# Causal term of the decay arguments on VectorE from head 2 on, and the sample tile's final scaling behind two bank reads

## The chip, the cores and the metric

The kernel runs on one core of a Trainium2 chip. The metric is the device time of one execution in microseconds (us). Of the engines, TensorE (PE in the profile) does matmuls and transposes into eight PSUM banks, VectorE (DVE) and ScalarE (ACT) read those banks, GpSimd (POOL) works on SBUF and issues DMAs, and SyncE (SP) issues most other DMAs. Each engine runs its instructions in program order, and semaphores order the engines among each other.

## The reference, cut to what matters

One step of a hybrid decoder layer: a short gated convolution and an mLSTM matrix memory read the same normalised input and write through one output projection. 2048 prompt tokens (with 16 meta tokens in front) and 64 sample tokens (8 sequences of 8) go through it. The change touches the decay weights of the mLSTM:

```python
log_d = jnp.where(causal, b[..., :, None] - b[..., None, :] + ig[..., None, :], -jnp.inf)
m_t = jnp.maximum(m_inter, jnp.max(log_d, axis=-1))
d = jnp.exp(log_d - m_t[..., None])
inter = jnp.exp(m_inter - m_t)
s = jnp.einsum('bhjd,bhsd->bhjs', q, k) * d
num = jnp.einsum('bhjs,bhsv->bhjv', s, v) + inter[..., None] * jnp.einsum('bhjd,bhdv->bhjv', q, c_prev)
```

and the last normalisation of the sample output:

```python
out = jnp.einsum('btw,wd->btd', jnp.concatenate([y_conv, y_m], axis=-1), w_out)
y_sample = rmsnorm(x + out, final_norm_gain)
```

## The kernel before, in words

**Stages.** A prologue transposes and splits the input. The main part goes over 4 heads (`g` = 0 to 3), each with 4 blocks (`b` = 0 to 3) of 512 tokens (4 chunks of 128); `n = 4 g + b` counts the blocks. "Head 2" is `g` = 1. In a block, nine tiles of projection columns follow each other in the order K, V, Q, GC, HC, GB, ZC, O, ZM. A tile is 24 matmuls of 512 columns, since both operands are split into two f16 parts and three products are taken for each of 8 slices (lines 732 to 734). V is built from 96 matmuls of 128 columns (lines 741 to 743). With `b` = 0 a small mixed piece (meta and sample tokens, 80 columns) comes ahead of each tile.

**Decay factors.** At the end of tile Q, TensorE writes into bank `A` the product of a row selector `selneg` and `mparts` (the running maximum in three bf16 parts, line 849), adds the causal mask on top by a second matmul (`identb` times the mask `maskb`, line 850), and writes the first product once more, without the mask, into bank `N[0]` (line 853). ScalarE makes `dp` = exp(A + column 3 of `sel`) and `eh` = exp(N[0] + column 4), four instructions each, one for a chunk. VectorE then multiplies `eh` by `qf`. At the end of the next tile, GC, TensorE writes the scores into bank `S` (line 860) and VectorE multiplies `dp` by them. From the middle of tile ZC on, TensorE takes the chunks (lines 809, 810 and 815) that need both. `dp` has held the block before's head output until then: it may be overwritten once GpSimd has made its four sums of it (semaphore `y_sums`, line 603).

**The end of the program.** After the last block, TensorE multiplies the sample rows by the output weights (lines 965, 966) into banks `T1` and `PB[0]`, and then does the prompt's output projection: 8 units of 256 rows, each with seven products of 12 matmuls (lines 978 to 980; a Strassen form with the operand sums S1 to S4). In unit 0 the order is A11 of unit 0, S2, S1, A12, S3, A11 of unit 1, A22, S4. A product goes into one of three banks of a chain, `one`, `two`, `three`. S3 adds to bank `two` what S2 left there, after VectorE has read it (`add_bank(..., s6_out, ...)`, which also waits for the first of three additions that GpSimd makes in `residuals`). A22 waits for `u7_out` in the same way, S4 for `c22_out`.

VectorE adds the sample banks to `zsmp` (four instructions), then takes the mean of squares of the sample tile (`b_mean(0, ...)`, after ScalarE's `b_square`), waits for GpSimd's power of -0.5 (`b_power(0, ...)`) and scales (`b_final(0, ...)`), and only then turns to unit 0. GpSimd's own order there is: the four sums of the last block, `residuals(0)`, `store_sums`, two small stores, `b_power(0, ...)`, a wait for `b_out`, the store of `y_sample`, and then `residuals(1)`.

VectorE and ScalarE issue through a helper, so all their instructions show as line 160; they are told apart by their tiles.

Of the kernel before, what the change touches and what calls it, by code (L numbers as in the profile page):

```python
# [33 lines left out]
ALU = mybir.AluOpType  # L34
ACT = mybir.ActivationFunctionType

P = 128
# [4 lines left out]
DB, DS = 8, 8  # L42
# [121 lines left out]
def build(nc, x_prompt, x_sample, state_conv, state_c, state_n, state_m, meta, norm_gain, w_in, conv_w,  # L164
# [3 lines left out]
    with ctx:  # L168
# [5 lines left out]
        def sem(name):  # L174
            return ctx.enter_context(nc.semaphore(name))
# [88 lines left out]
        def w_pair(w, t):  # L264
# [25 lines left out]
        t0_full, t0_free, t1_full, t1_free = sem("t0_full"), sem("t0_free"), sem("t1_full"), sem("t1_free")  # L290
        a_full, a_free, s_full, s_free = sem("a_full"), sem("a_free"), sem("s_full"), sem("s_free")
        e_full, e_ready, n_full, n_free = sem("e_full"), sem("e_ready"), sem("n_full"), sem("n_free")
        g_logits, g_abs, g_exp, g_ln, rows_ready = (
            sem(n) for n in ("g_logits", "g_abs", "g_exp", "g_ln", "rows_ready"))
        sel_ready, q_scaled, gc_used = sem("sel_ready"), sem("q_scaled"), sem("gc_used")
# [429 lines left out]
        def _(pe):  # L725
# [113 lines left out]
            def at_end(g, b, t, first):  # L839
                n = nth(g, b)  # L840
                if first:
                    for r in X_END.get(t, ()):
                        x_round(1 + CH * (b + 1) + r // 2, r % 2, t0(g, b, ("x", r), first))
                if t == Q:

                    pe.wait_ge(sel_ready, n + 1)
                    pe.wait_ge(a_free, n * 3)
                    m = mparts[:, tok0(b):tok0(b) + BT]
                    mm(A[:, :], selneg[:, :], m, start=True, stop=False)
                    mm(A[:, :], identb[:, :], maskb[:, :].unsqueeze(1).broadcast_to([P, CH, P]), start=False, stop=True)\  # L850
                        .then_inc(a_full, 1)
                    pe.wait_ge(n_free, n)
                    mm(N[0][:, :], selneg[:, :], m, start=True, stop=True).then_inc(e_full, 1)
                if t == GC:
                    bank_, left = evacuations(g, b, Q)
                    pe.wait_ge(p_free[bank_], left + 1)
                    pe.wait_ge(s_free, n * 3)
                    for c in range(CH):
                        cc = slice(c * P, (c + 1) * P)
                        last = mm(S[:, cc], kf[:, cc], qf[:, cc], start=True, stop=True)  # L860
                    last.then_inc(s_full, 1)
                if t == ZC:
                    chunk(g, b, 1, first)
                if t == O:
                    chunk(g, b, 3, first)
                if b == 0:
                    mixed_end(g, b, t, first)
                if b == 1 and t in (V, Q, GC):
                    i0, i1 = SAMPLE_ROUNDS[t - V]
                    pe.wait_ge(mx_v_wide, g + 1)  # L870
                    use_t1(t1(g, b, ("state", t - V), first))
                    mm(T1[:, 0:(i1 - i0) * DV1], kwm[:, :], v1x[:, i0:i1, :].rearrange("p b v -> p (b v)"),
                       start=True, stop=True).then_inc(t1_full, 1)
                if first and t == ZC:
                    gates(2 + 2 * CH * (b + 2), tok0(b + 1), BT, t1(g, b, "gates", first))
                if first and b == NB - 2 and t == ZM:
                    columns(b + 3, BT, t1(g, b, "next cols", first))
# [149 lines left out]
        def _(act):  # L1027
# [149 lines left out]
            def at_end(g, b, t, first):  # L1177
                n = nth(g, b)
                if t == Q:
                    act.wait_ge(ym_low, n)  # L1180
                    act.wait_ge(y_sums, 4 * n)
                    act.wait_ge(sel_ready, n + 1)

                    for out, src, kind, full, free, value in ((dp, A, 3, a_full, a_free, n * 3 + 1),
                                                              (eh, N[0], 4, e_full, e_ready, n + 1)):
                        act.wait_ge(full, value)
                        for c in range(CH):
                            cc = slice(c * P, (c + 1) * P)
                            last = fn(out[:, cc], src[:, cc], ACT.Exp, bias=sel[:, c, kind:kind + 1])
                            if c < CH - 1:  # L1190
                                did(last)
                        mark(last.then_inc(free, 1), free, value)
# [147 lines left out]
        def _(dve):  # L1340
# [242 lines left out]
            def select(g, b, first):  # L1583

                n = nth(g, b)
                if first and b == 0:
                    dve.wait_ge(const2, 1)
                if first or b == NB - 1:
                    dve.wait_ge(t1_free, COLS_COUNTS[b + 1] + 1)
                dve.wait_ge(tile_done, n * NT + 1)  # L1590
                dve.wait_ge(e_ready, n)
                if b == 0:
                    factors(g)
                mark(pick(sel[:, :, :], cols[:, 1 + CH * b:1 + CH * (b + 1), :, bass.ds(g, 1)].rearrange("p c k o -> p c (k o)"))
                     .then_inc(sel_ready, 1), sel_ready, n + 1)
# [11 lines left out]
            def at_end(g, b, t, first):  # L1607
# [1 line left out]
                if t == K and not first:  # L1609
                    select(g, b, first)  # L1610
                if t == Q:
                    dve.wait_ge(e_ready, n + 1)
                    mark(tt(eh[:, :], eh[:, :], qf[:, :], ALU.mult).then_inc(q_scaled, 1), q_scaled, n + 1)
                if t == GC:
                    dve.wait_ge(s_full, n * 3 + 1)
                    dve.wait_ge(a_free, n * 3 + 1)
                    mark(tt(dp[:, :], dp[:, :], S[:, :], ALU.mult).then_inc(s_free, 1), s_free, n * 3 + 1)
                if t == ZC:
                    dve.wait_ge(a_free, n * 3 + 2)
# [181 lines left out]
            def b_mean(tile, n):  # L1801

                dve.wait_ge(b_sq, tile + 1)
                mark(ts(msx[0:n, tile:tile + 1], ssx[0:n, tile:tile + 1], 1.0 / D, EPS, ALU.mult, ALU.add).then_inc(b_ms, 1), b_ms, tile + 1)

            def b_final(tile, z, n):

                dve.wait_ge(b_rs, tile + 1)
                mark(stt(z, z, rsx[0:n, tile:tile + 1], fgain[0:n, :], ALU.mult, ALU.mult).then_inc(b_out, 1), b_out, tile + 1)
# [6 lines left out]
            for h in range(2):  # L1816
# [2 lines left out]
                add_bank(z, SMP[h][0:n, :], smp_added, 2 * h + 1)  # L1819
                dve.wait_ge(smp_added, 2 * h + 1)  # L1820
                add_bank(z, SMP[h][n:2 * n, :], smp_added, 2 * h + 2)
            b_mean(0, n)
            dve.wait_ge(fg_in, 16)
            b_final(0, zsmp[0:n, :], n)
            for n in range(UNITS):
                z1, z2 = Z[n % 2]
                one, two, three = CHAINS[n % 2]
# [3 lines left out]
                if n:  # L1831
                    b_mean(2 * n, P)
                    b_final(2 * n - 1, Z[1 - n % 2][1], P)
                if n < UNITS - 1:
                    dve.wait_ge(prod_done, p2_done(n))
                    add_bank(z1[:, 0:BT], one[:, :], c11_out, n + 1)
# [7 lines left out]
                if n == UNITS - 1:  # L1844
                    dve.wait_ge(prod_done, p2_done(n))
                    add_bank(z1[:, 0:BT], one[:, :], c11_out, n + 1)
                dve.wait_ge(prod_done, p4_done(n))
                add_bank(z2[:, 0:BT], two[:, :], c21_out, n + 1)
                b_mean(1 + 2 * n, P)
# [42 lines left out]
```

## Time and profile before

| | |
|---|---|
| median of 3 runs | 1156.07 us (1153.03 to 1157.19) |
| the profiled execution's own time | 1155.46 us |
| its span | 1153.7 us |
| TensorE busy | 1095.1 us, 95% |
| VectorE busy | 519.4 us, 45% |
| ScalarE busy | 354.1 us, 31% |
| GpSimd busy | 249.9 us, 22% |

Engine times are from one profiled execution. The span runs from its first to its last recorded work, and the execution's own time is 1.76 us longer. A matmul's duration holds the fill and drain of the array, which overlap the next matmul: the distance from one start to the next is what it takes of the engine. The clock that TensorE was granted is given as a share of full speed.

### The profile page before, as it was taken

To read this page: it belongs to the slowest core of one execution; us is meant where nothing else is said; L and a number is where in the kernel's file an instruction comes from. 1 tells how busy PE (TensorE), PEld (TensorE's weight loads), DVE (VectorE), ACT (ScalarE), POOL (GpSimd) and SP (SyncE) were. 2 spreads that over 40 slices of the span, in tenths; PEclk is the share of its full clock that TensorE was granted. 3 is DMA by queue.
4 is the path that set the end of the run, shared out by engine and by line. 5 is a ranking of instruction groups with operands and counts; after the bars stand their busy time and mean duration, and the time that the engine had idled before them with its cause. 6 is when DMAs were issued, how large, how long until landed. Compare 5 with 4: busy or idle time off the path is not lost. (4 is left out here: it accounts for less than half of the span.)

```text
span 1153.7 us, 18272 instructions
## 1 busy us (share of the span) xinstructions
PE 1095.1 (95%) x7274; PEld 622.3 (54%) x7274; DVE 519.4 (45%) x1045; ACT 354.1 (31%) x701; POOL 249.9 (22%) x332
## 2 busy tenths in 40 slices
PE   3888999989999999999999999999999999799996
PEld 3555645545566555556565655566656555344442
DVE  5756665575533443454343424544432223334333
ACT  5563354625321323243222223422222131121211
POOL 5000220202020223120213131211211121433322
PEclk9989999999999999999999999999999999899998
DMA  5231020005220021173101314410212062246652
GB/s 179 76 109 43 12 92 23 29 23 136 82 83 7 16 87 61 47 198 87 38 7 48 87 43 125 139 35 20 91 37 88 23 210 88 103 146 229 220 209 90
DMA packets 89048, 100.02 MB, mean 87 GB/s; under 512 B 7248, under 2 KB 73956, under 8 KB 88964
## 3 DMA queue, kind: packets, MB, share of 16 engines
q1 hardware_dynamic: 49024, 58.06, 15.7%
q0 software_dynamic: 7600, 25.03, 6.0%
q10 hardware_dynamic: 32340, 15.78, 5.1%
q8 instruction: 57, 0.93, 0.3%
q14 instruction: 27, 0.22, 0.1%
HBM read 65.43 MB, written 33.41 MB: 86 GB/s over the span
## 5 line engine op out<-in xcount | busy, mean ns | idle before, releaser
L733 PE MATMUL bank<-xTl,Wh 128*128 128x512 f16 (+1 forms) x1280 | 420.9, 345 | 0.0
L732 PE MATMUL bank<-xTh,Wh 128*128 128x512 f16 (+1 forms) x1280 | 418.2, 345 | 2.4 <-DVE xtmp L160 2.4
L734 PE MATMUL bank<-xTh,Wl 128*128 128x512 f16 (+1 forms) x1280 | 420.2, 345 | 0.0
L734 PEld LDWEIGHTS bank<-xTh,Wl 128*128 128x128 f16 x1280 | 126.5, 99 | 121.9 <-issue 1.9
L732 PEld LDWEIGHTS bank<-xTh,Wh 128*128 128x128 f16 x1280 | 126.4, 99 | 110.7 <-issue 4.5
L733 PEld LDWEIGHTS bank<-xTl,Wh 128*128 128x128 f16 x1280 | 126.5, 99 | 108.9 <-issue 3.1
L741 PE MATMUL bank<-Wh,xTh 128*128 128x128 f16 x544 | 94.1, 221 | 4.2 <-DVE ysum L160 3.9
L743 PE MATMUL bank<-Wh,xTl 128*128 128x128 f16 x544 | 94.1, 221 | 0.0
L742 PE MATMUL bank<-Wl,xTh 128*128 128x128 f16 x544 | 94.1, 221 | 0.0
L160 ACT ACTIVATE tz<-bank 128x512 f32<-128x512 f32 x32 | 19.1, 598 | 134.7 <-PE bank L734 133.9
L160 DVE SCALAR_TENSOR_TENSOR Wl<-wst,Wh 128x1024 f16<-128x1024 f32 x36 | 46.1, 1282 | 29.1 <-ACT Wh L160 26.9
L741 PEld LDWEIGHTS bank<-Wh,xTh 128*128 128x128 f16 x544 | 53.7, 99 | 7.6 <-DVE ysum L160 5.4
L610 POOL TENSOR_TENSOR ysumst<-ysum,ysumst 128x1024 f16<-128x1024 f32 x16 | 34.1, 2132 | 95.2 <-ACT ysumst L160 95.2
L742 PEld LDWEIGHTS bank<-Wl,xTh 128*128 128x128 f16 x544 | 53.7, 99 | 1.6
L743 PEld LDWEIGHTS bank<-Wh,xTl 128*128 128x128 f16 x544 | 53.7, 99 | 0.0
L594 POOL DMA_DIRECT2D y_ops<-yst x16 | 11.8, 738 | 187.4 <-DVE yst L160 187.4
L160 DVE SCALAR_TENSOR_TENSOR cn<-cn,sel,bank 128x129 f32<-128x129 f32 x64 | 22.4, 350 | 62.9 <-PE bank L815 59.0
L160 DVE SCALAR_TENSOR_TENSOR xs<-bank,xs 128x512 f32<-128x512 f32 x36 | 24.9, 692 | 52.8 <-PE bank L980 52.1
L160 DVE TENSOR_TENSOR eh<-eh,qf 128x512 f32<-128x512 f32 x16 | 11.1, 692 | 80.9 <-ACT eh L160 80.9
L592 POOL DMA_DIRECT2D y_ops<-yst x16 | 11.9, 743 | 161.3 <-DVE yst L160 161.3
L160 ACT ACTIVATE Wh<-wst 128x1024 f16<-128x1024 f32 x36 | 38.0, 1057 | 26.4 <-PE bank L734 18.4
L763 PE MATMUL bank<-ident,xs 128*128 128x128 f32 (+1 forms) x136 | 24.7, 323 | 20.1 <-DVE xs L160 10.0
(313 smaller groups left out, 1602.1 us busy)
## 6 DMA issues: line engine op xcount, KB each, us to landing
xs<-in_x_prompt SPq DMA_DIRECT2D x28, 512.0 KB, 3.9
wst<-in_w_in ACTq DMA_DIRECT2D x27, 512.0 KB, 4.6
y_ops<-ysumst POOLq DMA_DIRECT2D x16, 512.0 KB, 3.2
w_ops<-xs SPq DMA_DIRECT2D x16, 448.0 KB, 3.8
out<-xs POOLq DMA_DIRECT2D x11, 512.0 KB, 2.9
Wh<-y_ops SPq DMA_DIRECT2D x12, 448.0 KB, 3.5
Wl<-y_ops SPq DMA_DIRECT2D x12, 448.0 KB, 4.3
wst<-in_w_in SPq DMA_DIRECT2D x9, 512.0 KB, 4.2
```

Source lines behind the costliest of these rows:

```text
L160: return op(*operands, **named)
L592: pool.dma_start(ops[:, :, A12 * 2 * P:(A22 + 1) * 2 * P], src).then_inc(out, 16)
L594: pool.dma_start(ops[:, :, 0:2 * P], src[:, :, 0:2 * P]).then_inc(out, 16)
L610: pool.tensor_tensor(parts[:, :, 1, :], ysum[:, :, :, :].rearrange("p r o t -> p (r o) t"), parts[:, :, 0, :], ALU.subtract).then_inc(y_su ...
L732: mm(out, wh[:, k, :], xh, start=(k == 0), stop=False)
L733: mm(out, wh[:, k, :], xl, start=False, stop=False)
L734: last = mm(out, wl[:, k, :], xh, start=False, stop=(k == KT - 1))
L741: mm(out, xh, Wh[:, V, k, :], start=(k == 0), stop=False)
L742: mm(out, xh, Wl[:, V, k, :], start=False, stop=False)
L743: last = mm(out, xl, Wh[:, V, k, :], start=False, stop=(k == KT - 1))
L763: last = nc.tensor.transpose(bank_[:, k * n:k * n + n], xs[unit % XBUF][0:n, (4 * r + k) * P:(4 * r + k + 1) * P], ident[0:n, 0:n])
```

## The change

Three things change. For `g` >= 1 the mask matmul and the second matmul of `selneg` go: TensorE writes only the plain product into bank `A`. VectorE adds the mask to it and writes the sum to `dp` in SBUF (a new semaphore, `arg_ready`). ScalarE then makes `eh` first, from bank `A`, and `dp` second, in place from SBUF (a new semaphore, `dp_ready`). Head 1 (`g` = 0) keeps the old form. VectorE rather than ScalarE now waits for `y_sums` there. At the end of the program, `b_mean(0, ...)` moves behind the read of bank `two` of unit 0, and `b_final(0, ...)` behind that unit's three other reads `c11_out`, `u7_out` and `c22_out`.

```diff
--- before.py
+++ after.py
@@ -290,6 +290,7 @@
         t0_full, t0_free, t1_full, t1_free = sem("t0_full"), sem("t0_free"), sem("t1_full"), sem("t1_free")
         a_full, a_free, s_full, s_free = sem("a_full"), sem("a_free"), sem("s_full"), sem("s_free")
         e_full, e_ready, n_full, n_free = sem("e_full"), sem("e_ready"), sem("n_full"), sem("n_free")
+        arg_ready, dp_ready = sem("arg_ready"), sem("dp_ready")
         g_logits, g_abs, g_exp, g_ln, rows_ready = (
             sem(n) for n in ("g_logits", "g_abs", "g_exp", "g_ln", "rows_ready"))
         sel_ready, q_scaled, gc_used = sem("sel_ready"), sem("q_scaled"), sem("gc_used")
@@ -846,11 +847,14 @@
                     pe.wait_ge(sel_ready, n + 1)
                     pe.wait_ge(a_free, n * 3)
                     m = mparts[:, tok0(b):tok0(b) + BT]
-                    mm(A[:, :], selneg[:, :], m, start=True, stop=False)
-                    mm(A[:, :], identb[:, :], maskb[:, :].unsqueeze(1).broadcast_to([P, CH, P]), start=False, stop=True)\
-                        .then_inc(a_full, 1)
-                    pe.wait_ge(n_free, n)
-                    mm(N[0][:, :], selneg[:, :], m, start=True, stop=True).then_inc(e_full, 1)
+                    if g:
+                        mm(A[:, :], selneg[:, :], m, start=True, stop=True).then_inc(a_full, 1)
+                    else:
+                        mm(A[:, :], selneg[:, :], m, start=True, stop=False)
+                        mm(A[:, :], identb[:, :], maskb[:, :].unsqueeze(1).broadcast_to([P, CH, P]), start=False, stop=True)\
+                            .then_inc(a_full, 1)
+                        pe.wait_ge(n_free, n)
+                        mm(N[0][:, :], selneg[:, :], m, start=True, stop=True).then_inc(e_full, 1)
                 if t == GC:
                     bank_, left = evacuations(g, b, Q)
                     pe.wait_ge(p_free[bank_], left + 1)
@@ -1177,13 +1181,18 @@
             def at_end(g, b, t, first):
                 n = nth(g, b)
                 if t == Q:
-                    act.wait_ge(ym_low, n)
-                    act.wait_ge(y_sums, 4 * n)
                     act.wait_ge(sel_ready, n + 1)
-
-                    for out, src, kind, full, free, value in ((dp, A, 3, a_full, a_free, n * 3 + 1),
-                                                              (eh, N[0], 4, e_full, e_ready, n + 1)):
-                        act.wait_ge(full, value)
+                    if g:
+                        act.wait_ge(arg_ready, n + 1 - NB)
+                    else:
+                        act.wait_ge(ym_low, n)
+                        act.wait_ge(y_sums, 4 * n)
+                        act.wait_ge(a_full, n * 3 + 1)
+
+                    for out, src, kind, free, value in ((eh, A, 4, a_free, n * 3 + 1), (dp, dp, 3, dp_ready, n + 1 - NB)) if g else (
+                            (dp, A, 3, a_free, n * 3 + 1), (eh, N[0], 4, e_ready, n + 1)):
+                        if src is N[0]:
+                            act.wait_ge(e_full, n + 1)
                         for c in range(CH):
                             cc = slice(c * P, (c + 1) * P)
                             last = fn(out[:, cc], src[:, cc], ACT.Exp, bias=sel[:, c, kind:kind + 1])
@@ -1588,7 +1597,10 @@
                 if first or b == NB - 1:
                     dve.wait_ge(t1_free, COLS_COUNTS[b + 1] + 1)
                 dve.wait_ge(tile_done, n * NT + 1)
-                dve.wait_ge(e_ready, n)
+                if n <= NB:
+                    dve.wait_ge(e_ready, n)
+                else:
+                    dve.wait_ge(dp_ready, n - NB)
                 if b == 0:
                     factors(g)
                 mark(pick(sel[:, :, :], cols[:, 1 + CH * b:1 + CH * (b + 1), :, bass.ds(g, 1)].rearrange("p c k o -> p c (k o)"))
@@ -1609,11 +1621,21 @@
                 if t == K and not first:
                     select(g, b, first)
                 if t == Q:
-                    dve.wait_ge(e_ready, n + 1)
+                    if g:
+                        dve.wait_ge(a_full, n * 3 + 1)
+                        dve.wait_ge(y_sums, 4 * n)
+                        mark(tt(chunks(dp[:, :]), chunks(A[:, :]), maskb[:, :].unsqueeze(1).broadcast_to([P, CH, P]), ALU.add)
+                             .then_inc(arg_ready, 1), arg_ready, n + 1 - NB)
+                        dve.wait_ge(a_free, n * 3 + 1)
+                    else:
+                        dve.wait_ge(e_ready, n + 1)
                     mark(tt(eh[:, :], eh[:, :], qf[:, :], ALU.mult).then_inc(q_scaled, 1), q_scaled, n + 1)
                 if t == GC:
                     dve.wait_ge(s_full, n * 3 + 1)
-                    dve.wait_ge(a_free, n * 3 + 1)
+                    if g:
+                        dve.wait_ge(dp_ready, n + 1 - NB)
+                    else:
+                        dve.wait_ge(a_free, n * 3 + 1)
                     mark(tt(dp[:, :], dp[:, :], S[:, :], ALU.mult).then_inc(s_free, 1), s_free, n * 3 + 1)
                 if t == ZC:
                     dve.wait_ge(a_free, n * 3 + 2)
@@ -1819,9 +1841,7 @@
                 add_bank(z, SMP[h][0:n, :], smp_added, 2 * h + 1)
                 dve.wait_ge(smp_added, 2 * h + 1)
                 add_bank(z, SMP[h][n:2 * n, :], smp_added, 2 * h + 2)
-            b_mean(0, n)
             dve.wait_ge(fg_in, 16)
-            b_final(0, zsmp[0:n, :], n)
             for n in range(UNITS):
                 z1, z2 = Z[n % 2]
                 one, two, three = CHAINS[n % 2]
@@ -1831,6 +1851,8 @@
                 if n:
                     b_mean(2 * n, P)
                     b_final(2 * n - 1, Z[1 - n % 2][1], P)
+                else:
+                    b_mean(0, DB * DS)
                 if n < UNITS - 1:
                     dve.wait_ge(prod_done, p2_done(n))
                     add_bank(z1[:, 0:BT], one[:, :], c11_out, n + 1)
@@ -1844,6 +1866,8 @@
                 if n == UNITS - 1:
                     dve.wait_ge(prod_done, p2_done(n))
                     add_bank(z1[:, 0:BT], one[:, :], c11_out, n + 1)
+                if n == 0:
+                    b_final(0, zsmp[0:DB * DS, :], DB * DS)
                 dve.wait_ge(prod_done, p4_done(n))
                 add_bank(z2[:, 0:BT], two[:, :], c21_out, n + 1)
                 b_mean(1 + 2 * n, P)
```

TensorE, end of tile Q in the last block of the last head. Before:

```order
L734 MATMUL bank<-xTh,Wl 128x512
L849 MATMUL bank<-mparts,selneg 128x512
L850 MATMUL bank<-maskb,identb 128x512
L853 MATMUL bank<-mparts,selneg 128x512
L732 MATMUL bank<-xTh,Wh 128x512
L733 MATMUL bank<-xTl,Wh 128x512
```

And now, where every line number of TensorE is one or two higher:

```order
L735 MATMUL bank<-xTh,Wl 128x512
L851 MATMUL bank<-mparts,selneg 128x512
L733 MATMUL bank<-xTh,Wh 128x512
L734 MATMUL bank<-xTl,Wh 128x512
L735 MATMUL bank<-xTh,Wl 128x512
```

Two of the three matmuls between tile Q and tile GC are gone; nothing else moved on TensorE.

VectorE, tiles V to GC of the last block, as a piece of the difference (`maskb` is the mask):

```order
 L160 TENSOR_TENSOR yst<-dp,yst 128x4x128
 L160 TENSOR_TENSOR kw<-bank,sel 128x512
+L160 TENSOR_TENSOR dp<-bank,maskb 128x512
 L160 TENSOR_TENSOR eh<-eh,qf 128x512
 L160 TENSOR_TENSOR dp<-dp,bank 128x512
```

One instruction was added, between the scaling of K and the product with Q.

VectorE, from the last head output on (`wst` 64x... is the sample tile, `xs` the output rows of unit 0, `prow` the small outputs). Before:

```order
L160 MEMSET den 128x1
L160 SCALAR_TENSOR_TENSOR wst<-bank,wst 64x512 x4
L160 TENSOR_SCALAR msx<-ssx 64x1
L160 SCALAR_TENSOR_TENSOR wst<-wst,rsx,fgain 64x1024
L160 SCALAR_TENSOR_TENSOR xs<-bank,xs 128x512 x5
L160 TENSOR_SCALAR msx<-ssx 128x1
L160 SCALAR_TENSOR_TENSOR xs<-bank,xs 128x512
```

And now:

```order
L160 MEMSET den 128x1
L160 SCALAR_TENSOR_TENSOR wst<-bank,wst 64x512 x4
L160 SCALAR_TENSOR_TENSOR xs<-bank,xs 128x512
L160 TENSOR_SCALAR msx<-ssx 64x1
L160 SCALAR_TENSOR_TENSOR xs<-bank,xs 128x512 x3
L160 SCALAR_TENSOR_TENSOR wst<-wst,rsx,fgain 64x1024
L160 SCALAR_TENSOR_TENSOR xs<-bank,xs 128x512
L160 TENSOR_SCALAR msx<-ssx 128x1
```

The mean of the sample tile now stands behind the first bank read of unit 0, and its scaling behind the fourth.

## Rows read from the trace of the kernel before

**Rows 1.** The page, part 1: busy us, share of the span, instructions.

```profile
PE 1095.1 (95%) x7274; PEld 622.3 (54%) x7274; DVE 519.4 (45%) x1045; ACT 354.1 (31%) x701; POOL 249.9 (22%) x332
```

**Rows 2.** Busy us (instructions) in a stretch: PE, PEld, DVE, ACT, POOL, clock, DMA.

```profile
520.00:740.00 220.00, 218.84 (x1563) 128.07 (x1562) 91.04 (x192) 65.14 (x137) 49.05 (x57) 1.00 0.24 72
```

**Rows 3.** Waits of TensorE: us in total, times, longest.

```profile
PE bank L978 <- DVE xs L160: 7.0, 1, 7.0
...
PE bank L790 <- DVE dp L160: 1.7, 2, 1.2
```

**Rows 4.** Timeline of TensorE, a Q end: start, us, engine, line.

```profile
944.12 0.38 PE L849 MATMUL bank<-mparts,selneg 68*128 68x512 bf16 x1
...
944.56 0.38 PE L853 MATMUL bank<-mparts,selneg 68*128 68x512 bf16 x1
944.78 0.38 PE L732 MATMUL bank<-xTh,Wh 128*128 128x512 f16 x1
```

**Rows 5.** Line 850 from 300 to 960 us: ns min/median/max, first and last.

```profile
L850 PE MATMUL bank<-maskb,identb x12: 379/379/380, 333.0 to 944.3; 128*128 128x512 bf16 x12
```

**Rows 6.** Timeline of an ordinary block (head 2, third block), by engine.

```profile
448.24 1.57 ACT L160 ACTIVATE dp<-bank,sel 128x128 f32<-128x128 f32 x4
...
451.50 0.69 DVE L160 TENSOR_TENSOR eh<-eh,qf 128x512 f32<-128x512 f32 x1 [5.87 <-ACT eh L160]
454.26 0.69 DVE L160 TENSOR_TENSOR dp<-dp,bank 128x512 f32<-128x512 f32 x1 [2.06 <-PE bank L860]
...
467.01 0.39 PE L809 MATMUL bank<-v,dp 128*128 128x129 f32 x2
```

**Rows 7.** Timeline of head 2's fourth block, by engine.

```profile
503.41 1.57 ACT L160 ACTIVATE dp<-bank,sel 128x128 f32<-128x128 f32 x4 [2.63 <-POOL ysum L603]
...
509.09 0.60 ACT L160 ACTIVATE gcs<-bank 128x512 f32<-128x512 f32 x1
...
509.20 0.69 DVE L160 TENSOR_TENSOR dp<-dp,bank 128x512 f32<-128x512 f32 x1
...
511.89 0.38 PE L732 MATMUL bank<-xTh,Wh 128*128 128x512 f16 x1
...
519.66 0.39 PE L809 MATMUL bank<-v,dp 128*128 128x129 f32 x2
```

**Rows 8.** Timeline of TensorE around the end's longest wait.

```profile
998.63 0.38 PE L980 MATMUL bank<-xTh,Wl 128*128 128x512 f16 x1
1005.98 0.61 PE L978 MATMUL bank<-xTh,Wh 128*128 128x512 f16 x1 [6.96 <-DVE xs L160]
...
1010.19 0.38 PE L978 MATMUL bank<-Wh 128*128 128x512 f16 x1
...
1012.78 0.38 PE L978 MATMUL bank<-xTh,Wh 128*128 128x512 f16 x1
```

**Rows 9.** Timeline of VectorE in the same stretch.

```profile
991.08 3.06 DVE L160 SCALAR_TENSOR_TENSOR wst<-bank,wst 64x512 f32<-64x512 f32 x4
997.37 0.15 DVE L160 TENSOR_SCALAR msx<-ssx 64x1 f32<-64x1 f32 x1 [3.23 <-ACT junk L160]
1003.82 1.27 DVE L160 SCALAR_TENSOR_TENSOR wst<-wst,rsx,fgain 64x1024 f32<-64x1024 f32 x1 [6.30 <-POOL rsx L685]
1005.23 1.49 DVE L160 SCALAR_TENSOR_TENSOR xs<-bank,xs 128x512 f32<-128x512 f32 x2
```

**Rows 10.** Timeline of GpSimd in the same stretch.

```profile
995.09 3.72 POOL L680 TENSOR_TENSOR xs<-xs,xtmp 128x512 f32<-128x512 f32 x3
998.76 2.13 POOL L610 TENSOR_TENSOR ysumst<-ysum,ysumst 128x1024 f16<-128x1024 f32 x1
...
1003.12 0.60 POOL L685 TENSOR_TENSOR rsx<-msx,halves 64x1 f32<-64x1 f32 x1
1005.40 0.60 POOL L702 DMA_DIRECT2D out<-wst  x1 [1.68 <-DVE wst L160]
```

**Rows 11.** As in rows 2, a stretch behind the long wait.

```profile
1005.00:1010.00 5.00, 4.02 (x12) 1.50 (x13) 1.48 (x3) 0.00 (x0) 0.60 (x1) 0.57 0.24 52
```

## The prediction

> **What bounds the kernel now.** I read the page's busy shares first. TensorE is busy for 1095.1 of 1153.7 us, VectorE for under half [rows 1]. An average can hide a stage with another limit, so I took the busy times by stage next: in 520 to 740 us TensorE is busy for 218.84 of 220 us at full granted clock, VectorE for 91.04 [rows 2]. In heads 2 to 4 the time is therefore what TensorE has to issue, and an instruction taken from it should come back whole. Then the list of TensorE's waits: apart from the first 300 us, which the change leaves as they are, it holds two short ones of together 1.7 us (line 790, for `dp`), and one of 7.0 us, the longest of all, in front of a product of line 978 [rows 3]. That one is the second place where time can be had. The timelines of three engines around it say what it waits for.
>
> **Part 1, two matmuls less in each block of heads 2 to 4.** Line 850 ran 12 times in those heads [rows 5], line 853 once beside it each time, so 24 matmuls go. What one takes of TensorE is the distance between starts: from 944.12 (line 849) two starts on to 944.56 (line 853) and one more to 944.78, so 0.22 us each, not the 0.38 us in the duration column [rows 4]. 24 x 0.22 = 5.3 us. Charging the duration would give 24 x 0.38 = 9.1 us; I leave that out of the range's centre because the next matmul started while the last was still draining.
>
> The Trainium skill ("TensorE: Matmul & The Clock Gate", "Wait — 56ns, not 53.3ns?") puts back-to-back matmuls of 512 columns at 215.7 ns from start to start. As an estimate by that page the 24 would be 5.2 us; the same page's duration of a matmul would not be the price.
>
> **What VectorE gets for it.** Twelve additions `dp<-bank,maskb` of 128x512. The trace has none with a mask operand in bf16; the nearest row is the product `dp<-dp,bank` of the same size, also with one PSUM operand, at 0.69 us [rows 6]. That is 12 x 0.69 = 8.3 us of VectorE in all. In an ordinary block it stood idle for 5.87 us ahead of `eh<-eh,qf` [rows 6], and the addition lies in exactly that idle time. Even at three times 0.69 us it would fit. Cost on the path: 0, bound above only by the cover below.
>
> **The new order of hands.** Before: ScalarE made `dp` (1.57 us) and `eh` (as long), and VectorE went on at 451.50, 3.26 us after ScalarE's start at 448.24 [rows 6]. Now: addition 0.69, `eh` 1.57, and VectorE can go on, while ScalarE makes `dp` for another 1.57. With ScalarE's start at 448.24 as before (the addition runs while it still copies Q out), `eh` times `qf` comes at about 449.9 instead of 451.5, and `dp` is ready at about 451.6. The product with the scores stood at 454.26, released by TensorE [rows 6], so it does not move. Its first user, line 809, started at 467.01, that is 12.1 us after the product's end at 454.95 [rows 6].
>
> The tighter case is the fourth block of heads 2 and 3, where GpSimd is late with its sums and ScalarE waited 2.63 us for them before `dp` at 503.41 [rows 7]. There the addition can't start before 503.4, so ScalarE starts 0.7 to 0.8 us later than before, and so does all behind it in its queue: a weight split, a copy of sums, and `gcs<-bank` at 509.09 to 509.69. The last of them frees the bank that tile GB needs; GB started at 511.89 [rows 7]. The copy would end at 510.5, so 1.4 us are left, 1.0 us when TensorE is 0.44 us earlier. VectorE's product with the scores would slip from 509.20 to about 510, still 9 us ahead of line 809 at 519.66 [rows 7]. Cost: 0; if that cover were gone, two blocks x 0.8 us = 1.6 us at most. The two waits of line 790 hang on VectorE's work since the end of the block before, not on the Q end, and stay at 1.7 us [rows 3]. They could also hide one block's gain each, so I put part 1 between 5.3 - 1.6 = 3.7 us and 5.3 us and take 5.3.
>
> The Trainium skill ("PSUM — Partial Sum Buffer", "PSUM bank collisions raise a hardware error") says that two engines must not read one bank in the same partitions at once. Bank `A` now has two readers, so they must stand in a row, and `arg_ready` puts them so. By that rule the 0.7 us of the addition can't be overlapped with `eh`. That waiting is what rival B below lives on: without the rule it would have no chance at all, with it a small one. No run here shows such a collision.
>
> **Part 2, the sample tile's scaling.** TensorE's last matmul before the wait started at 998.63 and would have let the next one start at 998.85. It started at 1005.98 [rows 8]: 7.13 us lost. VectorE is the reason. Its four sample additions ended at 994.14. It waited 3.23 us for ScalarE's squares, took the mean at 997.37, waited 6.30 us for GpSimd's power, scaled from 1003.82 to 1005.09, and read the bank for S3 only at 1005.23 [rows 9]. GpSimd was late because its power stood behind `residuals(0)` (995.09 to 998.81), `store_sums` (998.76 to 1000.89) and stores, and ran at 1003.12 [rows 10].
>
> Now the bank read comes first. It needs S2, which ended two products of 2.59 us before 998.85, so at 993.7, and the first of GpSimd's three additions, 995.09 + 3.72/3 = 996.33 [rows 10]. A product at full speed takes 1012.78 - 1010.19 = 2.59 us [rows 8]. The read runs from about 996.4 to 997.2 (0.75 us, half of the pair at 1005.23 [rows 9]). TensorE wants it at 998.85, so 1.6 us are left over, and the wait goes.
>
> What is late next? After the gap the twelve matmuls of S3 took 1010.19 - 1005.98 = 4.21 us instead of 2.59 [rows 8], because a good part of them ran at the lower of the two granted clock levels, 1.2 instead of 2.4 GHz: the clock of 1005 to 1010 us is a mean of 0.57 of full speed, and the first matmul shows 0.61 us instead of 0.38 [rows 8, 11]. Without the gap nothing lets the clock fall: another 1.62 us. Part 2 is then 7.13 + 1.62 = 8.75 us. The next waits: S3 ends at 1001.44, VectorE reads for A22 until 1002.4 and for S4 until 1003.2, and TensorE wants them at 1004.03 and 1006.62 (A11 of unit 1 lies between), so no wait. The sample scaling then waits for the power at 1003.72 and runs to 1005.1, before A22 ends at 1006.6: hidden. GpSimd issues the store of the sample rows behind it (0.60 us [rows 10]) and is free for `residuals(1)` at 1005.9; the first of its additions ends at 1007.1, and the read that needs it can't come before S2 of unit 1 ends, five products of 2.59 us after 998.85, at 1011.8. About 4.7 us are left.
>
> The Trainium skill ("TensorE: Matmul & The Clock Gate", "Part 1: The HAM clock gate (the "warmup" mystery)") says that the length of the slow stretch after a pause varies from run to run with where the pause falls. By that rule the 1.62 us is one draw, and in the median run the gain of part 2 could be 7.1 us plus less or more than that; the profiled run alone can't tell.
>
> **The sum.** 5.3 + 8.75 = 14.0 us. Against the profiled execution's own 1155.46 us that is 1141.4; that execution is 0.61 us under the median of 1156.07, against which it is 1142.0. I forecast 1141.8 us.
>
> **Rivals.**
> A: the wait at the end only changes its name. For: S3 needs GpSimd too, and its margin is 1.6 us, on a queue where four sums stand ahead of `residuals(0)`. Against: GpSimd's rows there don't depend on anything that the change moves. If all of part 2 were lost, 5.3 us would be left: 1150.5 us.
> B: VectorE's longer chain eats part 1. For: the late blocks. Against: 12.1 and 9 us of cover. Then 8.75 us are left: 1147.0 us.
> C: slower. The point from which it decides is the cover ahead of line 809 in an ordinary block: 2.7 us from `dp` ready at 451.6 to the product with the scores, and 12.1 us behind that. If addition, `eh` and `dp` in a row were longer by more than 14.8 us, each microsecond beyond it would stop TensorE in 10 blocks. To reach 1162 us, 20 us would have to be lost, 2 us in each of them: the addition would take 14.8 + 2 + 0.7 = 17.5 us in place of 0.69. No row comes near it.
> D: the change does not do what it says, for example if the stop of line 978 was not VectorE's read but something else that came last. Then 1150 us or above, with A's price. The semaphore `s6_out` and the row at 1005.23 speak against it; I count it with A.
>
> **How the numbers follow.** Forecast 0.88, A with D 0.05, B 0.05, C 0.02. A measurement of this kernel can tell about 0.5%, 5.8 us, from no change. Forecast and B are faster by more than that; A, at 5.6 us under the median, is just within it. So faster 0.93, same 0.05, slower 0.02. The forecast's own range: from part 1 at 3.7 and part 2 at 7.13 (11 us, 1145) to the full 14.0, with the 2 us by which single runs of before lay around their median: 1139.5 to 1145.5 us. That leaves about 2 in 10 outside, most of it the other cases.
>
> **What would show it.** In the profile after: TensorE's wait list without the 7.0 us at line 978's successor; 24 matmuls less; S3's twelve matmuls at 2.59 us; the sample scaling behind four reads and ahead of TensorE's next need; VectorE's idle time ahead of `eh<-eh,qf` turned into a wait for bank `A`, the addition of 0.69 us and a shorter wait. Busy TensorE from 300 to 960 us should drop by 5.3 us in length and keep its share. Wrong would be: a new wait of TensorE for `gcs`, for `dp`, or for GpSimd's `xs`; an addition of over 1 us; or a clock under 1.00 between 990 and 1010 us.

## Result: 1140.8 us, ratio 0.987

| | before | after |
|---|---|---|
| median | 1155.92 us (4 runs) | 1140.84 us (4 runs, 1138.38 to 1141.35) |
| ratio | | 0.9869 (95% interval 0.9845 to 0.9892) |
| profiled execution, own time | 1155.46 us | 1141.35 us |
| span | 1153.7 us | 1139.6 us |

The kernel became 15.1 us faster by the medians and 14.1 us by the two profiled executions. The prediction had 1141.8 us, and 1141.4 us for an execution like the profiled one.

The page of the changed kernel, part 1, answers to [rows 1]:

```profile
PE 1088.8 (96%) x7250; PEld 620.0 (54%) x7250; DVE 529.7 (46%) x1057; ACT 355.7 (31%) x701; POOL 250.0 (22%) x332
```

24 matmuls are gone and 12 instructions of VectorE have come. The list of TensorE's waits from 300 us on, which answers to [rows 3], has lost the one of 7.0 us:

```profile
PE bank L791 <- DVE dp L160: 1.4, 2, 0.7
```

TensorE at the Q end, as in [rows 4] (columns: start, us, engine, line): one matmul in 0.22 us where three took 0.66.

```profile
939.21 0.38 PE L851 MATMUL bank<-mparts,selneg 68*128 68x512 bf16 x1
939.43 0.38 PE L733 MATMUL bank<-xTh,Wh 128*128 128x512 f16 x1
```

The ordinary block of [rows 6], VectorE and then ScalarE of the changed kernel:

```profile
447.14 0.69 DVE L160 TENSOR_TENSOR dp<-bank,maskb 128x512 f32<-128x512 f32 x1 [2.12 <-PE bank L851]
449.51 0.69 DVE L160 TENSOR_TENSOR eh<-eh,qf 128x512 f32<-128x512 f32 x1 [1.69 <-ACT eh L160]
453.21 0.69 DVE L160 TENSOR_TENSOR dp<-dp,bank 128x512 f32<-128x512 f32 x1 [3.00 <-PE bank L864]
```

```profile
447.91 1.57 ACT L160 ACTIVATE eh<-bank,sel 128x128 f32<-128x128 f32 x4 [0.40 <-DVE dp L160]
449.51 1.70 ACT L160 ACTIVATE dp<-dp,sel 128x128 f32<-128x128 f32 x4
```

The idle time of 5.87 us ahead of `eh<-eh,qf` has become a wait of 2.12 us for bank `A`, the addition, and a wait of 1.69 us. The product with the scores is still released by TensorE.

The end, as in [rows 8 to 10]; first VectorE, then TensorE, then GpSimd:

```profile
991.21 0.69 DVE L160 SCALAR_TENSOR_TENSOR xs<-bank,xs 128x512 f32<-128x512 f32 x1 [2.41 <-PE bank L984]
992.03 0.15 DVE L160 TENSOR_SCALAR msx<-ssx 64x1 f32<-64x1 f32 x1
...
996.29 1.49 DVE L160 SCALAR_TENSOR_TENSOR xs<-bank,xs 128x512 f32<-128x512 f32 x2 [1.90 <-PE bank L984]
998.42 1.28 DVE L160 SCALAR_TENSOR_TENSOR wst<-wst,rsx,fgain 64x1024 f32<-64x1024 f32 x1 [0.63 <-POOL rsx L686]
1001.47 0.69 DVE L160 SCALAR_TENSOR_TENSOR xs<-bank,xs 128x512 f32<-128x512 f32 x1 [1.78 <-PE bank L984]
```

```profile
993.29 0.38 PE L984 MATMUL bank<-xTh,Wl 128*128 128x512 f16 x1
993.50 0.38 PE L982 MATMUL bank<-xTh,Wh 128*128 128x512 f16 x1
```

```profile
1000.61 1.28 POOL L681 TENSOR_TENSOR xs<-xs,xtmp 128x512 f32<-128x512 f32 x1
```

The bank read ends at 991.90, and S3 starts at 993.50 right behind the product ahead of it, so 1.6 us were to spare. The sample scaling lies between the fourth read and the fifth, whose matmuls it doesn't hold up.

**Where the time came from.** I cut each trace at four marks: the first matmul of line 849 (851 after) in head 2, the last one in head 4, the start of unit 0's first product, and the last start of line 978 (982 after).

| us | first mark at | heads 2 to 4, to the second | to the third | products, to the fourth | rest |
|---|---|---|---|---|---|
| before | 332.8 | 611.3 | 44.4 | 153.2 | 12.0 |
| after | 333.1 | 606.1 | 43.9 | 144.5 | 12.0 |
| difference | +0.3 | -5.2 | -0.4 | -8.7 | 0 |

The differences are rounded after the subtraction. The third stretch holds the Q end of the last block, and so two of the 24 matmuls: together the matmul part gave 5.6 us.

### The profile page after: what moved, and what is told of

Same layout as the page of the kernel before. It is cut to its first block and busy times, and to the rows that moved or that the text cites. A ratio compares the mean times of both kernels' runs of the same rounds, so it can differ in the third digit from the quotient of the medians.

```text
span 1139.6 us, 18225 instructions
## 1 busy us (share of the span) xinstructions
PE 1088.8 (96%) x7250; PEld 620.0 (54%) x7250; DVE 529.7 (46%) x1057; ACT 355.7 (31%) x701; POOL 250.0 (22%) x332
## 5 line engine op out<-in xcount | busy, mean ns | idle before, releaser
L658 POOL TENSOR_TENSOR hrs<-hms,halves 128x4 f32<-128x4 f32 x16 | 16.5, 1032 | 112.6 <-DVE hms L160 112.6
```

Of the source, the lines that this page charges most:

```text
L658: pool.tensor_tensor(hrs[:, :], hms[:, :], halves[:, :], ALU.pow).then_inc(h_rs, 1)
```

## Experiments

Every kernel ran beside the kernel before on the same chip, on three chips in all. Each ratio is to that kernel's runs there (medians 1153.0, 1154.7 and 1154.4 us), and the differences in us below go by the ratios; "heads" and "products" are the stretches of the table above.

### The two parts alone

`tail_only` is the kernel before with part 2 alone:

```diff
-            b_mean(0, n)
             dve.wait_ge(fg_in, 16)
-            b_final(0, zsmp[0:n, :], n)
@@ behind the read of unit 0 for S3
+                else:
+                    b_mean(0, DB * DS)
@@ behind the reads for A22 and S4
+                if n == 0:
+                    b_final(0, zsmp[0:DB * DS, :], DB * DS)
```

> The kernel before with part 2 alone: the sample tile's mean and scaling behind the bank reads, all matmuls kept. Theory (the two parts add up, 7.13 us of wait and 1.62 us of low clock): 8.75 us less, 1147.2 us against 1155.9 of the kernel before. Rival A (GpSimd or another wait takes its place): above 1152 us. If the clock's 1.6 us does not come back: 1148.8 us. In the profile TensorE has no wait in front of S3 and its twelve matmuls take 2.6 us.

Measured: 1144.18 us, ratio 0.9927 (0.9910 to 0.9944), 8.4 us less. Heads 611.5, products 144.5, the same as after. Nothing took the place of the wait.

`mask_only` is the changed kernel with those lines put back as they were:

```diff
+            b_mean(0, n)
             dve.wait_ge(fg_in, 16)
+            b_final(0, zsmp[0:n, :], n)
@@
-                else:
-                    b_mean(0, DB * DS)
@@
-                if n == 0:
-                    b_final(0, zsmp[0:DB * DS, :], DB * DS)
```

> The changed kernel without part 2: two matmuls less in each of twelve blocks, VectorE adds the mask; the sample tile is scaled ahead of the bank reads as before. Theory (TensorE's issue is the bound, 0.216 us a matmul): 5.2 to 5.7 us less than the kernel before, 1150.4 us. Rival B (VectorE's longer chain eats it): 1154 to 1156 us. If a matmul cost its duration of 0.38 us: 9.1 us less, 1146.8 us.

Measured: 1149.11 us, ratio 0.9964 (0.9950 to 0.9978), 4.2 us less. Heads 606.3 and the third stretch 0.4 us less, so 5.4 us came from the matmuls. The products took 154.35 us, 1.1 more than the 153.25 before. The pause ahead of S3 is the same, 7.1 us, but the granted clock of 0.50 lasted until 5.5 us into the work behind it, and until 3.3 us into it in the profile before. TensorE, S3's first matmul and the first of the next product:

```profile
998.01 0.61 PE L982 MATMUL bank<-xTh,Wh 128*128 128x512 f16 x1 [6.95 <-DVE xs L160]
...
1003.11 0.60 PE L982 MATMUL bank<-Wh 128*128 128x512 f16 x1
```

S3 took 5.10 us here and 4.21 in [rows 8], 2.59 at full clock. The two parts add up to 12.6 us by the ratios; their intervals reach to the 14 to 15 us of the whole. In the traces, where the clock's draw can be set apart, they are 5.4 and 8.7 us.

### What the price of a matmul is

`more_matmuls`: the changed kernel with eight more of the same matmul at each Q end of heads 2 to 4.

```diff
                     if g:
+                        for _ in range(8):
+                            mm(A[:, :], selneg[:, :], m, start=True, stop=True)
                         mm(A[:, :], selneg[:, :], m, start=True, stop=True).then_inc(a_full, 1)
```

> The changed kernel with eight more matmuls of the same 512 columns into bank A at the end of tile Q in heads 2 to 4 (96 in all; each overwrites the last, so the output stays). If a matmul costs the distance between starts, 0.216 us: 20.7 us more than the changed kernel, 1161.5 us. If it costs its duration of 0.38 us: 36.5 us more, 1177.3 us. If other engines set part of the time: clearly under 20 us more.

Measured: 1162.23 us, ratio 1.006 (1.0041 to 1.0079), 22 us above the changed kernel. Heads 628.7, that is 22.6 us more, of which 2.0 are the longer waits below (1.4 us in the changed kernel); 20.6 are left for the matmuls. 20.7 us were expected from the distance between starts, 36.5 from the duration.

```profile
PE bank L791 <- DVE dp L160: 3.4, 2, 2.5
```

### What stopped TensorE at the end

`mean_ahead`: the changed kernel with `b_mean(0, ...)` ahead of the reads again, only `b_final(0, ...)` behind them.

```diff
+            b_mean(0, n)
             dve.wait_ge(fg_in, 16)
@@
-                else:
-                    b_mean(0, DB * DS)
```

> The changed kernel with only the scaling of the sample tile behind the bank reads; its mean of squares (which waits for ScalarE) stands ahead of them as before. Before, VectorE waited 3.2 us for ScalarE's squares and 6.3 us for GpSimd's power. If the wait for the power alone is what stopped TensorE: the same time as the changed kernel, 1140.8 us, since the mean would end at about 0.7 us before the time at which the read must start. If the squares' wait counts too: a wait of TensorE of up to 1 us and 1141 to 1142 us, more if the clock falls as well.

Measured: 1139.09 us, ratio 0.9882 (0.9868 to 0.9896); products 144.5. VectorE:

```profile
989.50 0.14 DVE L160 TENSOR_SCALAR msx<-ssx 64x1 f32<-64x1 f32 x1 [3.22 <-ACT junk L160]
989.78 0.69 DVE L160 SCALAR_TENSOR_TENSOR xs<-bank,xs 128x512 f32<-128x512 f32 x1
```

The read runs from 989.78 to 990.47, and S3 starts at 990.98 without a wait. Only the wait for GpSimd's power stopped TensorE; moving the mean was not needed.

`fill_wait`: the kernel before with 30 matmuls, whose result nobody uses, in the wait.

```diff
+                if n == 0:
+                    pe.wait_ge(t0_free, t0(H, 0, "hT", False) - t0_uses(0, False).index("hT") + 1)
+                    for i in range(30):
+                        mm(T0[:, :], yops[0][i % H][:, 0:P], w_operand(xTh, i % H, B_11), start=True, stop=True)
                 pe.wait_ge(s6_out, n + 1)
```

> The kernel before with 30 idle matmuls into the free bank T0 ahead of S3 of unit 0 (30 x 0.216 = 6.5 us in a wait of 7.13 us); their result is used by nobody. The wait itself stays. Theory (1.62 us of the 8.75 us are the low clock behind the pause): S3's twelve matmuls take 2.6 us and the time falls by 1.6 us to 1154.3 us. Rival (the low clock has another cause, or costs nothing on the path): 1155.9 us, no change.

Measured: 1153.53 us, ratio 0.9986 (0.9975 to 0.9998); products 151.6 instead of 153.2. TensorE, the last filler, S3's first and the next product's first:

```profile
1002.72 0.38 PE L1012 MATMUL bank<-Wh,Wl 128*128 128x512 f16 x1
1003.58 0.39 PE L978 MATMUL bank<-xTh,Wh 128*128 128x512 f16 x1 [0.49 <-DVE xs L160]
...
1006.18 0.38 PE L978 MATMUL bank<-Wh 128*128 128x512 f16 x1
```

S3 takes 2.60 us, so 1.6 us of part 2 were the clock and 7.1 the wait itself.

`power_first`: the kernel before, GpSimd's power moved up.

```diff
             residuals(0)
+            b_power(0, DB * DS)
             store_sums(H - 1, NB - 1)
@@
-            b_power(0, DB * DS)
             pool.wait_ge(b_out, 1)
```

> The kernel before with GpSimd's power of the sample tile moved ahead of its sums' store and two small stores (it runs at about 998.8 instead of 1003.1 us). VectorE's order is as before. Theory (the wait is VectorE's queue behind GpSimd's queue): the scaling runs from 999.5 to 1000.8, the read until 1001.6, so TensorE waits some 2.8 us instead of 7.1: 4.3 us less. If the clock stays up over the shorter pause, 1.6 us more of gain: 1150.0 us; if it still falls: 1151.6 us. Rival (something else releases S3): 1155.9 us.

Measured: 1153.35 us, ratio 0.9981 (0.9968 to 0.9994), 2.2 us less, where 4.3 were expected; products 151.4, 1.9 less. VectorE and then GpSimd:

```profile
999.61 3.06 DVE L160 SCALAR_TENSOR_TENSOR wst<-wst,rsx,fgain 64x1024 f32<-64x1024 f32 x1 [1.91 <-POOL rsx L685]
```

```profile
999.49 2.11 POOL L610 TENSOR_TENSOR ysumst<-ysum,ysumst 128x1024 f16<-128x1024 f32 x1
```

The power came early, but the scaling took 3.06 us beside GpSimd's subtraction instead of 1.27 [rows 9]. TensorE still stood idle for 4.5 us (2.8 expected), and S3 took 4.93 us, 0.7 more than before, at the low clock.

`power_alone` moves GpSimd's wait for the scaled tile and that tile's store up with the power, so that GpSimd is idle meanwhile:

```diff
             residuals(0)
+            b_power(0, DB * DS)
+            pool.wait_ge(b_out, 1)
+            pool.dma_start(y_sample.rearrange("b t d -> (b t) d"), zsmp[0:DB * DS, :]).then_inc(smp_store, 16)
             store_sums(H - 1, NB - 1)
```

> The kernel before with GpSimd's power of the sample tile, its wait for the scaled tile and that tile's store moved ahead of the sums' store, so that GpSimd does nothing while VectorE scales. In the run with the power alone moved, VectorE's scaling took 3.06 instead of 1.27 us while GpSimd worked on its sums (2.11 us). Theory (the two engines hold each other up over SBUF): the scaling takes 1.3 us again, TensorE waits some 2.7 us instead of 7.1, and 4.0 us (clock falls) to 6.1 us (clock stays) are gained on the kernel before. Rival (the scaling is slow there for another reason, such as its place behind the power): 3.06 us again, 1.9 us gained.

Measured: 1149.50 us, ratio 0.9965 (0.9951 to 0.9978), 4.0 us less; products 148.9. VectorE's scaling and then TensorE:

```profile
996.92 1.28 DVE L160 SCALAR_TENSOR_TENSOR wst<-wst,rsx,fgain 64x1024 f32<-64x1024 f32 x1 [1.91 <-POOL rsx L685]
```

```profile
999.08 0.39 PE L978 MATMUL bank<-xTh,Wh 128*128 128x512 f16 x1 [2.57 <-DVE xs L160]
...
1000.39 0.63 PE L978 MATMUL bank<-xTh,Wh 128*128 128x512 f16 x1
...
1003.80 0.38 PE L980 MATMUL bank<-Wh 128*128 128x512 f16 x1
```

The scaling is back at 1.28 us, so the 3.06 came from GpSimd's work beside it. Behind the pause of 2.7 us the clock still fell, here only 1.3 us after TensorE had gone on.

### How much room the addition had

`add_x5` (and `add_x3` with 2 in place of 4):

```diff
+                        for _ in range(4):
+                            did(tt(chunks(dp[:, :]), chunks(A[:, :]), maskb[:, :].unsqueeze(1).broadcast_to([P, CH, P]), ALU.add))
```

> The changed kernel with VectorE's addition of the mask done five times over in each block of heads 2 to 4 (48 more additions of 0.69 us, about 3.2 us more a block; same result). The prediction's cover was line 809 with 14.8 us in ordinary blocks, and 0.8 to 1.0 us in front of tile GB in the two late blocks. Theory 1 (that cover): ordinary blocks lose nothing, the two late ones 2.4 us each, 4.7 us more, 1145.5 us. Theory 2 (ScalarE's copy of GC frees a bank for tile GB with 4.8 us of cover in every block): the same 1145.5 us here, but see twelve additions. Theory 3 (VectorE's time bounds): 38 us more.

Measured: 1151.22 us, ratio 0.9973 (0.9961 to 0.9984), about 12 us above the changed kernel; heads 617.8, that is 11.7 more. TensorE's waits from 300 to 1000 us:

```profile
PE bank L893 <- ACT ehm L160: 4.2, 3, 1.4
PE bank L733 <- ACT gcs L160: 3.8, 2, 1.9
PE bank L876 <- DVE cs L160: 1.9, 3, 0.7
PE bank L791 <- DVE dp L160: 1.5, 2, 0.8
```

All three theories missed. Five additions took 3.59 us in place of 0.69, so each block had 2.9 us more. From start to start of TensorE, a late block lost 2.0 us of them ahead of line 733, which leaves 0.9 us of room, near the 1.0 predicted. But two covers that the prediction had not looked at gave way as well: each first block lost 1.6 us ahead of line 893 and each second block 0.8 us ahead of line 876. (The list's own waits are up to 0.2 us shorter than the distances between starts.) In a first block ScalarE has the exponentials of the mixed tile behind `dp`, and they free the bank that line 893 needs:

```profile
340.86 0.28 PE L893 MATMUL bank<-ident,kfm 128*80 128x128 f32 x1 [1.41 <-ACT ehm L160]
```

> The changed kernel with the addition of the mask done three times in each block of heads 2 to 4 (1.45 us more a block). The prediction said that three times would fit without cost in ordinary blocks. With five times (2.9 us more) the trace showed TensorE waiting 1.4 us in each first block for ScalarE's exp of the mixed tile, 1.9 us in the two late blocks for the copy of GC, and 0.6 us in second blocks for VectorE's state updates, 11.7 us in all over heads 2 to 4. Theory 1 (covers of 1.5, 1.0 and 2.3 us): only the late blocks lose, 0.5 us each, so 1 us more than the changed kernel. Theory 2 (the cost is in proportion to the addition): 5.8 us more.

Measured: 1142.21 us, ratio 0.9891 (0.9874 to 0.9907), 2 us above the changed kernel on the same chip, with intervals that overlap; heads 608.0, 1.9 more. In the list only the late blocks' wait is new:

```profile
PE bank L791 <- DVE dp L160: 1.6, 2, 0.9
PE bank L733 <- ACT gcs L160: 0.9, 2, 0.4
```

From start to start, each late block lost 0.6 us (0.5 expected), each first block 0.1 us, where theory 1 has none, and the waits of line 791 were 0.2 us longer. With 1.45 us added a block, both this run and `add_x5` give 0.9 us of room in the late blocks and 1.3 in the first ones.

### Head 1 as well, and one more step

`all_heads`: each `if g` of the change made true for head 1 too, and the counts of the two semaphores raised by one head. On TensorE, for instance:

```diff
-                    if g:
+                    if True:
                         mm(A[:, :], selneg[:, :], m, start=True, stop=True).then_inc(a_full, 1)
@@ and on VectorE, in select
-                if n <= NB:
-                    dve.wait_ge(e_ready, n)
-                else:
-                    dve.wait_ge(dp_ready, n - NB)
+                dve.wait_ge(dp_ready, n)
```

> The changed kernel with head 1 in the new form as well: eight matmuls less, four additions of 0.69 us more on VectorE, in the stage in which TensorE waits for VectorE. Theory 1 (TensorE issue bounds there too): 1.7 us less than the changed kernel, 1139.1 us. Theory 2 (VectorE bounds head 1, since several of TensorE's waits between 60 and 300 us name it): the additions come late into those waits, up to 4 x 0.8 us more against 1.7 us less, 1140.8 to 1142.3 us.

Measured: 1142.09 us, ratio 0.9908 (0.9893 to 0.9922), 3.0 us above `mean_ahead` on the same chip, which differs from the changed kernel only in the place of the mean. Theory 1 is out, and theory 2 has the sign right, with a loss above its upper end of 1.5 us. TensorE's waits of 60 to 330 us sum to 20.6 us, those of `mean_ahead` (head 1 as before) to 17.2: 3.4 us more, against 1.7 us of matmuls saved, and head 2 starts 1.9 us later. The first of its list, which took 0.5 us there:

```profile
PE bank L764 <- ACT xs L160: 3.8, 2, 2.2
```

`changed_again` is the changed kernel once more, as the reference on the third chip.

> The changed kernel itself, beside the other kernels of this call and the kernel before: ratio 0.987, 14 to 15 us less. It gives the others their reference on this chip.

Measured: 1140.22 us, ratio 0.9876 (0.9859 to 0.9892).

`defer_split`: VectorE's split of the next head's first weight tile behind the head output.

```diff
                     at_half(g, b, t, first)
+                    if following == "weights" and t == V:
+                        split_w(g + 1, K)
@@
-                    if following == "weights":
+                    if following == "weights" and t != K:
                         split_w(g + 1, t)
```

> The changed kernel with VectorE's split of the next head's first weight tile placed behind the head output in the fourth block of each head, instead of ahead of it. TensorE waited 0.7 us there in heads 2 and 3 (line 791, for that head output). Theory: these waits go, 1.4 us less than the changed kernel, near the limit of what can be told. Rival (VectorE's later split delays ScalarE's loads and with them GpSimd's sums and the copy of GC, whose cover is 1.0 us): no change or up to 2 us more.

Measured: 1137.74 us, ratio 0.9857 (0.9844 to 0.9871). Heads 604.4, 1.7 us less than after, and TensorE's list from 310 to 1000 us is empty. The trace shows the gain; by the times it is the fastest of all, but its interval overlaps that of `changed_again`, so the total is not shown apart.

## Why the prediction was right

- **TensorE's issue is the bound in heads 2 to 4.** Right. 24 matmuls less gave 5.6 us between the marks. 5.3 were expected (5.2 at the unrounded 0.216 us a start); most of the rest is that the waits of line 790/791 sum to 1.4 us instead of 1.7, where the prediction had them unchanged. `mask_only` shows it alone, and `more_matmuls` shows that the price is the distance between starts.
- **The addition at 0.69 us, in VectorE's idle time.** Right: 12 instructions of 0.69 us.
- **`eh` times `qf` earlier, `dp` later.** Right. In the ordinary block, `eh` times `qf` starts 2.8 us after the first matmul into bank A (446.72), where it was 4.2 us (447.33): 1.4 us sooner, with 1.6 expected. The addition did not quite fit beside ScalarE's copy of Q: ScalarE stood idle for 0.40 us ahead of `eh`.
- **The late blocks, 1.0 us left.** Right to 0.1 us: `add_x5` and `add_x3` both give 0.9 us of room.
- **Cover in ordinary blocks, and rival C's deciding point.** Wrong, without effect on the time. The prediction named line 809 with 14.8 us. The runs give 1.3 us in first blocks (bank of the mixed tile, ScalarE's queue) and 2.1 us in second ones (VectorE's state updates). For the third blocks no run reached the limit. I had followed only what needs `dp`, and not what stands behind it in the queues. Three times the addition, which the prediction had fit into an ordinary block, fits in second and third blocks but costs 0.1 us in each first one. In head 1 four additions of 0.69 us came with 3.4 us more of waits (`all_heads`).
- **Part 2 is 7.13 us of wait and 1.62 us of clock.** Right: 8.7 us in the products, 1.6 of them shown to be the clock by `fill_wait`. The read was 1.6 us early, as worked out.
- **What is late next: nothing.** Right, line by line: the scaling at 998.42 before the fifth read, `residuals(1)` at 1000.61.
- **GpSimd's place in the cause.** Incomplete. The power stood behind other work, but moving it alone helps little (`power_first`), since the scaling then runs beside GpSimd's sums.
- **The clock's share is one draw.** Behind the same pause of 7.1 us, the slow stretch cost 1.6 us in the profile before and 2.7 us in `mask_only` (products of 154.35 us, less 144.50 and less the pause of 7.12). These two executions agree with what the prediction took from the Trainium skill ("TensorE: Matmul & The Clock Gate", "Part 1: The HAM clock gate (the "warmup" mystery)"), that the length of the slow stretch differs from run to run.
- **The total.** Its closeness is in part luck. The profiled execution was forecast at 1141.4 us and took 1141.35, but its head 2 started 0.3 us later than in the profile before, and it gained 0.3 us more than forecast from the matmuls, and four executions of the changed kernel lie between 1138.38 and 1141.35 us.

## What to carry to other kernels

Where one engine issues without a gap, an instruction taken from it is worth the distance between starts, and a neighbour with idle time in that very place can take it over. To find the cover of a step that gets longer, follow every instruction behind it in each queue to the bank it frees, not only the readers of its result. Small work of a side tile should stand behind the reads that the bound engine waits for, above all where it waits itself for a third engine.

## What the runs showed of the hardware

- GpSimd's work can hold VectorE up. VectorE's scaling of 64x1024 with two SBUF tensors took 3.06 us when it began 0.12 us after a GpSimd subtraction of 2.11 us (`power_first`), and 1.28 us with GpSimd idle (`power_alone`). The subtraction, which had begun first, took no longer than the 2.13 us of [rows 10]. The Trainium skill ("SBUF — State Buffer", "Who interferes with whom") says that a VectorE instruction with two SBUF inputs contends with a GpSimd instruction that reads SBUF, and that the one that comes later is blocked until the first is done. As an estimate by that rule and these rows, 2.11 - 0.12 + 1.28 = 3.27 us would follow; the measured 3.06 is 0.2 us less.
- ScalarE's exp of 128x128 took 401 ns from SBUF (`dp<-dp`) and 367 ns from a bank, four of them 1.70 and 1.57 us. The change pays that 48 times, 1.6 us, all hidden.
- The granted clock fell to the lower of its levels, 1.2 GHz, while TensorE stood idle for 7.1 us (before: 1.00 from 998.9 to 1002.4 us, 0.50 from 1002.5 to 1009.2; `mask_only`) and for 4.5 us (`power_first`). Behind the idle time of 2.7 us (`power_alone`) it fell only 1.3 us into the work that followed, and was 0.50 from 1000.4 to 1003.7 us.
- The start of head 2 lies between 329.9 us (`tail_only`) and 333.1 us (after) in single executions of kernels that do the same up to there. In 120 to 200 us the granted clock was 0.96 in the profile before and 1.00 in `fill_wait`. It may be a good part of the 4 us between single runs of one kernel; that was not tested.
